# Decoder layer kernel: where the opening loads go, and which engine sums the second half of shift and scale

## The reference

```python
mod = (silu(c) @ w_ada + b_ada)             # c: (1, 1024), w_ada: (1024, 6144)
shift1, scale1, gate1, shift2, scale2, gate2 = jnp.split(mod, 6, axis=-1)

h = rms_norm(x, pre_mix_w) * (1.0 + scale1) + shift1
proj = h @ w_in                             # w_in: (1024, 2312)
q, k, v, xs, z, bm, cm, dt_raw = _split_last(proj, IN_SPLITS)
attn = sliding_window_attention(q, k, v, rel_bias, attn_sinks)
ssm = mamba2_mixer(xs, z, bm, cm, dt_raw, ...)
x = x + gate1 * rms_norm(concat([attn, ssm]) @ w_out, post_mix_w)

h = rms_norm(x, pre_ffn_w) * (1.0 + scale2) + shift2
u = causal_dwconv(h @ w_up);  f = gelu(u_gate) * u_val
x = x + gate2 * rms_norm(f @ w_down, post_ffn_w)
```

## Time and profile before

| | us |
|---|---|
| three runs | 1161.8, 1159.23, 1161.77 |
| median | 1161.77 |
| the profiled execution | 1160.59 |
| its span, from the first to the last instruction | 1158.8 |
| TensorE busy (share of the span) | 1100.1 (95%) |
| VectorE busy | 863.1 (74%) |
| ScalarE busy | 536.2 (46%) |

### The profile page before, as it was taken

How to read it: one execution, slowest core, us unless ns; L and a number is a source line. 1 busy time by engine, 2 the same in 40 slices (tenths; PEclk the granted TensorE clock), 3 DMA queues, 4 the chain that set the end, 5 groups by cost and what they waited for, 6 DMA issues and landing times.

```text
span 1158.8 us, 14802 instructions
## 1 busy us (share of the span) xinstructions
PE 1100.1 (95%) x5176; PEld 895.5 (77%) x5176; DVE 863.1 (74%) x1089; ACT 536.2 (46%) x900; POOL 212.1 (18%) x203
## 2 busy tenths in 40 slices
PE   2699999999999999969999999999999999999997
PEld 2578877777787878757888888888888888888885
DVE  5779567657459566587988888888888886776687
ACT  3631144445444343466454444454445454454453
POOL 2100000000012333123333333333333100000012
PEclk7699999999999999988999999999999999999999
DMA  9989311001132111105344343434353496733224
GB/s 341 313 245 316 119 37 37 20 19 37 37 110 81 64 38 55 56 36 146 109 164 140 131 151 120 159 128 158 109 170 109 144 365 225 237 100 98 94 90 165
DMA packets 115293, 152.69 MB, mean 132 GB/s; under 512 B 15084, under 2 KB 75053, under 8 KB 115245
## 3 DMA queue, kind: packets, MB, share of 16 engines
q1 hardware_dynamic: 114925, 151.00, 38.8%
q0 software_dynamic: 320, 1.06, 0.3%
HBM read 121.10 MB, written 30.95 MB: 131 GB/s over the span
## 4 chain that ended last, share of the span: by engine, by line
PE 89%; DVE 4%; DMA 2%; ACT 2%; issue 1%; POOL 1%; SPq 1%; DVEq 0%; POOLq 0%; ACTq 0%
PE ps L2259 34%; PE ps L1912 25%; PE ps L2324 17%; PE ps L1978 2%; PE ps L1951 2%; PE ps L1965 1%; PE ps L2102 1%; PE ps L2017 1%; DVE big L1233 1%; DMA raw<-in_w_in_dram 1%; ACT big L956 1%; DMA scratch<-in_rel_bias_dram 1%; PE ps L2146 1%; PE ps L2194 1%; PE ps L2094 1%
## 5 line engine op out<-in xcount | busy, mean ns | idle before, releaser
L1912 PE MATMUL ps<-a_hi,w_hi 128*128 128x512 f32 x416 | 144.8, 426 | 8.0 <-DVE a_lo L1293 5.7
L1912 PE MATMUL ps<-a_lo,w_hi 128*128 128x512 f32 x416 | 132.4, 397 | 0.0
L1912 PE MATMUL ps<-a_hi,w_lo 128*128 128x512 f32 x416 | 131.3, 394 | 0.0
L2324 PE MATMUL ps<-w_hi,a_hi 128*128 128x512 f32 x308 | 119.9, 389 | 0.2 <-DVE a_lo L1745 0.2
L2324 PE MATMUL ps<-w_lo,a_hi 128*128 128x512 f32 x308 | 119.8, 389 | 0.0
L2324 PE MATMUL ps<-w_hi,a_lo 128*128 128x512 f32 x308 | 119.8, 389 | 0.0
L1145 ACT ACTIVATE w_hi<-raw 128x512 fp32r<-128x512 f32 x77 | 48.7, 632 | 98.4 <-PE ps L2324 88.3
L1912 PEld LDWEIGHTS ps<-a_hi,w_hi 128*128 128x128 f32 x416 | 73.2, 191 | 26.5 <-issue 16.3
L1912 PEld LDWEIGHTS ps<-a_hi,w_lo 128*128 128x128 f32 x416 | 79.2, 190 | 18.2
L1912 PEld LDWEIGHTS ps<-a_lo,w_hi 128*128 128x128 f32 x416 | 78.9, 190 | 17.9 <-issue 0.5
L1065 ACT ACTIVATE scratch<-ps 128x512 f32<-128x512 f32 x88 | 52.2, 593 | 84.8 <-PE ps L2259 84.8
(11 more groups left out here) (244 smaller groups left out, 2418.1 us busy)
## 6 DMA issues: line engine op xcount, KB each, us to landing
big<-in_w_ada_dram SPq DMA_DIRECT2D x24, 1024.0 KB, 8.8
raw<-in_w_up_dram SPq DMA_DIRECT2D x22, 512.0 KB, 5.1
big<-in_w_up_dram SPq DMA_DIRECT2D x22, 512.0 KB, 4.7
big<-in_w_down_dram SPq DMA_DIRECT2D x22, 512.0 KB, 6.4
down_weight_sums<-big SPq DMA_DIRECT2D x22, 512.0 KB, 3.4
raw<-down_weight_sums SPq DMA_DIRECT2D x44, 256.0 KB, 2.8
ffn_hidden<-big SPq DMA_DIRECT2D x21, 512.0 KB, 2.6
big<-ffn_hidden SPq DMA_DIRECT2D x21, 512.0 KB, 7.5
```

The source lines that it names most:

```text
L1912: mm = pe.matmul(out, lhs_of[a], rhs_of(b, j), start=first and p == 0, stop=last and p == 2)
L2324: mm = pe.matmul(bk, a[:, ts], rhs_op(s)[w], start=fresh and m == 0, stop=last and m == 2, skip_group_check=s // KH in (J6, J3, J7))
```

## The change

**Places.** The eight blocks of x get places of their own in `spare` (the space of `a_hi` and `a_lo`, tiles 0 to 3 of each), and chunks 0 to 3 get four places: two in `big` as before, for chunks 0 and 2, and two in `spare` (tiles 4 to 7 of `a_hi` and `a_lo`) for chunks 1 and 3. No load of the opening waits for a consumer any more. SyncE's order is: x 0, constants, x 1, c, flip matrix, x 2 and 3, chunk 0, x 4 to 7, the small vectors, chunk 2, unit 0's weights, chunk 1, unit 1's weights, chunk 3, and, once the first columns are in PSUM, chunks 4 and 5.

**Halves.** Chunks 0 and 2 hold shift1 and scale1 of features 0 to 511, which are tiles 0 to 3 of h; chunks 1 and 3 those of tiles 4 to 7. VectorE sums chunks 0 and 2 in full, and tiles 0 to 3 are modulated after them (`take_part(0, 0)`). Of chunks 1 and 3 VectorE sums only rows j = 0 to 3, after the low halves of tiles 0 to 3. TensorE does the other four rows itself in `chunk_rows`: the four `silu(c)` columns, each beside a column of zeros (`c_pad`), are the stationary operand, the chunk's 512 columns stream, and one more product adds VectorE's partial sum; chunk 1 ends in the first and chunk 3 in the second of two PSUM partitions. ScalarE copies the two rows out (`copy_row`), TensorE turns them into columns (`row_columns`), VectorE takes them (`take_part(0, 1)`).

**Order of the steps.** TensorE does steps 0 to 3 of unit 0, the rows, steps 0 to 3 of unit 1 (the small transposes behind step 0), then steps 4 to 7 of unit 0 and of unit 1. The bias flips stand before step 6 of unit 1, where they stood before step 2. All transposes of x come first. ScalarE loads its table with a Silu of a constant and takes x's first squares before `silu(c)`.

**Names.** Some semaphores are joined: x blocks share theirs with the reloads of f (eight instead of six), chunk halves with the last stage's weights, and the four token sums of the feed-forward stage share one.

```diff
-        chunk = [flat(big[:, 4 * s:4 * s + 4, :]).rearrange("p (j n) -> p j n", j=KT) for s in range(2)]
+        chunk = [flat(tiles).rearrange("p (j n) -> p j n", j=KT)
+                 for tiles in (big[:, 0:4, :], big[:, 4:8, :], spare[:, 4:8, :], spare[:, 12:16, :])]
 
         x1nT = big[:, 0:8, :]
 
         def x_in(b):
 
-            return (raw if b % 4 < 2 else gate_rows)[:, b % 2, :]
+            return spare[:, b if b < 4 else b + 4, :]
...
+        c_pad = dtv[:, 0, 0:3 * KT].rearrange("p (j v) -> p j v", v=3)
+        one_pad = dtv[:, 0, 3 * KT:3 * KT + 3]
+        mod_row = scratch[0:2, 0:1024].rearrange("p (h n) -> p h n", h=2)
...
             load_x(0)
+            sp.dma_start(sq[:, :], squares[:, 0:3 * P]).then_inc(s_const, 16)
             load_x(1)
             sp.dma_start(ca[:, 0, :], c.rearrange("o (p j) -> p (o j)", j=KT)).then_inc(s_const, 16)
-            sp.dma_start(sq[:, :], squares[:, 0:3 * P]).then_inc(s_const, 16)
             sp.dma_start(flip, squares[:, 3 * P:]).then_inc(s_const, 16)
+            for b in range(2, 4):
+                load_x(b)
             load_chunk(0)
-            load_x(2)
-            load_x(3)
+            for b in range(4, NB):
+                load_x(b)
...
+            load_chunk(2)
+            load_in(0)
             load_chunk(1)
-            load_x(4)
-            load_x(5)
-            load_chunk(2)
-            load_x(6)
-            load_x(7)
+            load_in(1)
             load_chunk(3)
...
-                if n < 2:
-                    sp.wait_ge(s_xT, 5 + n)
-                else:
-                    sp.wait_ge(s_wlo, n - 1)
+            load_chunk(4)
+            load_chunk(5)
+            for n in range(2, U_OUT):
+                sp.wait_ge(s_wlo, n - 1)
                 if n != U_DT:
                     load_in(n)
...
             pool.wait_ge(s_bd, 16)
+            pool.wait_ge(s_mp, 2)
...
+            for b in range(4):
                 x_squares(b)
-                if b >= 3:
-                    x_evacuate(b - 3)
-            x_evacuate(NB - 3)
-            x_evacuate(NB - 2)
-            split_hi(0)
+                if b == 2:
+                    act.wait_ge(s_const, 48)
+                    act.activation(ca[:, 1, :], ca[:, 0, :], ACT.Silu).then_inc(s_cs, 1)
+                    act.wait_ge(s_cs, 1)
+                    act.wait_ge(s_pool, 5)
+                    act.activation(c_pad[:, :, 1], ca[:, 1, :], ACT.Copy).then_inc(s_cz, 1)
+            for b in range(3):
+                x_evacuate(b)
+            for b in range(4, NB):
+                x_squares(b)
+                x_evacuate(b - 1)
...
+            def copy_row(half):
+
+                act.wait_ge(s_rw, half)
+                act.activation(mod_row[:, half, :], bank(4 + half)[0:2, :], ACT.Copy).then_inc(s_rc, 1)
+
...
             h_hi(0)
             h_modulate(1)
-            for k in range(2, KT, 2):
-                h_modulate(k + 1)
-                h_hi(k - 1)
-                h_hi(k)
-            h_hi(KT - 1)
+            h_modulate(3)
+            h_hi(1)
+            h_hi(2)
+            h_hi(3)
+            split_hi(1)
+            copy_row(1)
+            act.wait_ge(s_mod, 2)
+            h_hi(4)
+            h_modulate(5)
+            h_hi(5)
+            h_hi(6)
+            h_modulate(7)
+            h_hi(7)
...
-            normalise(0)
-            normalise(1)
+            LOW = range(KT // 2)
+            for b in range(4):
+                normalise(b)
             sum_chunk(0)
-
+            for b in range(4, NB):
+                normalise(b)
 
             dve.wait_ge(s_rT, 1)
             link(dve.tensor_copy(cols[:, :], bank(7)[:, 0:280]))
...
-
-            sum_chunk(1)
-            normalise(2)
-            normalise(3)
             sum_chunk(2)
-            normalise(4)
-            normalise(5)
-            normalise(6)
-            normalise(7)
-            sum_chunk(3)
             dve.wait_ge(s_cols, 1)
...
             modulate(xnT, 0, 0, 0, T, s_h)
             split_lo(0)
-            for k in range(KT):
-                if k % 2 == 0 and k + 2 < KT:
-                    modulate(xnT, k + 2, 0, 0, T, s_h)
-                dve.wait_ge(s_hhi, k + 1)
-                h_lo(xnT, k, 0, T, s_hlo)
+            modulate(xnT, 2, 0, 0, T, s_h)
+            for k in range(4):
+                low_tile(k)
+            sum_chunk(1, LOW)
+            split_lo(1)
+            sum_chunk(3, LOW)
+            dve.wait_ge(s_mp, 2)
+            take_part(0, 1)
+            dve.wait_ge(s_mod, 2)
+            modulate(xnT, 4, 0, 0, T, s_h)
+            modulate(xnT, 6, 0, 0, T, s_h)
+            for k in range(4, KT):
+                low_tile(k)
...
+            def chunk_rows(half, v):
+
+                n = half + 2 * v
+                slot = ada_slot(n)
+                row = bank(4 + half)[0:2, :]
+                col = slice(1 - v, 3 - v)
+                pe.wait_ge(s_wb[2 * slot + 1], ada_loaded(n))
+                pe.wait_ge(s_cz, 1)
+                for j in range(KT // 2, KT):
+                    pe.matmul(row, c_pad[:, j, col], chunk[slot][:, j, :], start=v == 0 and j == KT // 2, stop=False)
+                pe.wait_ge(s_acc, 2 * half + v + 1)
+                mm = pe.matmul(row, one_pad[:, col], acc[:, n * 512:(n + 1) * 512], start=False, stop=v == 1)
+                if v == 1:
+                    mm.then_inc(s_rw, 1)
+
+            def row_columns(half):
+
+                pe.wait_ge(s_rc, half)
+                for f in range(4):
+                    c0 = EXT + 8 * half + 2 * f
+                    mm = pe.transpose(bank(6)[:, c0:c0 + 2], mod_row[:, half, f * P:(f + 1) * P], ident[0:2, 0:2])
+                mm.then_inc(s_mp, 1)
...
+            pe.wait_ge(s_pool, 5)
+            for b in range(NB):
+                x_transpose(b)
 
             pe.wait_ge(s_small, 16 * N_SMALL)
...
-            x_transpose(4)
-            sum_columns(2, EXT + 8)
-            x_transpose(5)
-            x_transpose(6)
-            x_transpose(7)
-            sum_columns(3, EXT + 12).then_inc(s_mp, 1)
+            part_columns(0)
+            part_columns(1).then_inc(s_mp, 1)
...
+
+            pe.wait_ge(s_xe, NB)
+            for k in range(KT // 2):
+                pe.wait_ge(s_wlo, 1)
+                pe.wait_ge(s_hlo, k + 1)
+                unit_step(0, k)
+            chunk_rows(1, 0)
+            chunk_rows(1, 1)
+            pe.wait_ge(s_wlo, 2)
+            for k in range(KT // 2):
+                if k == 1:
+                    row_columns(1)
+                unit_step(1, k)
+            for n in range(2):
+                for k in range(KT // 2, KT):
+                    pe.wait_ge(s_hlo, k + 1)
+                    if n == 1 and k == KT - 2:
+                        bias_flip()
+                    mm = unit_step(n, k)
+                mm.then_inc(s_wu, 1)
+
+            for n in range(2, U_OUT):
                 pe.wait_ge(s_wlo, n + 1)
...
```

More of the change, by code:

```diff
@@ new lines, in _, with load_in @@
+            in_src = w_in2.rearrange("(k p) n -> p k n", p=P)
+            def load_in(n):
+                dst = ring(raw, n).rearrange("p (k n) -> p k n", k=KT)
+                c0 = COLUMN[n] * P
+                if n < K:
+                    for e in range(2):
+                        h = n + 4 * e
+                        sp.dma_start(dst[:, :, e * HD:(e + 1) * HD],
+                                     in_src[:, :, h * HD:(h + 1) * HD]).then_inc(s_w[n % 2], 16)
+                else:
+                    sp.dma_start(dst, in_src[:, :, c0:c0 + P]).then_inc(s_w[n % 2], 16)
@@ L678, in _ @@
             pool.wait_ge(s_pool, 3)
-            for b in range(2):
+            for b in range(NB):
                 x_rstd(b)
@@ L683, in _ @@
             pool.dma_start(bias_d, ext_sb).then_inc(s_bd, 16)
-            for b in range(2, NB):
-                x_rstd(b)
             pool.wait_ge(s_bd, 16)
+            pool.wait_ge(s_mp, 2)
             for e in range(2):
@@ L1249, in _, with take_part @@
             dve.tensor_copy(ext_sb, bank(6)[0:H, 0:EXT]).then_inc(s_exs, 1)
-            sum_chunk(1)
-            normalise(2)
-            normalise(3)
             sum_chunk(2)
-            normalise(4)
-            normalise(5)
-            normalise(6)
-            normalise(7)
-            sum_chunk(3)
-            dve.wait_ge(s_cols, 1)
+            dve.wait_ge(s_cols, 1)
+            def take_part(n, half):
+                a = 16 * n + 4 * half
+                sums = bank(6)[:, EXT + 8 * half:EXT + 8 * half + 8].rearrange("p (f v) -> p v f", v=2)
+                for v in range(2):
+                    c0 = a + 8 * v
+                    ins = dve.tensor_tensor(modc[:, c0:c0 + 4], sums[:, v, :], cols[:, 8 * n + c0:8 * n + c0 + 4],
+                                            ALU.add)
+                link(ins)
+                dve.scalar_tensor_tensor(out=modc[:, a + 8:a + 12], in0=modc[:, a + 8:a + 12],
```

(2 more changed lines are left out.)

191 lines of the change are left out of this document (95 added, 96 removed).

## The result

| | before | after |
|---|---|---|
| median of four runs, us | 1161.78 (1159.23 to 1162.37) | 1167.92 (1167.04 to 1168.59) |
| the profiled execution | 1160.59 | 1167.04 |
| its span | 1158.8 | 1165.2 |
| first product of unit 0 | 52.62 | 44.05 |
| last low half of h done | 63.45 | 72.31 |

The ratio is 1.0048, 95% interval 1.0036 to 1.006: slower, by 6.1 us between the medians and 6.4 between the spans of the profiled executions. The gate products are 6.2 later, so nearly the whole loss is made by then; from there to the end the two kernels take 1025.3 and 1025.5 us (1158.8 - 133.49 and 1165.2 - 139.69).

A forecast was written before the change was run, and what follows sets the result against it. TensorE, busy nearly all the time, was taken as the bound. The larger of +2.5 and +5.9 us moved the profiled 1160.59 to 1166.5; with the median 1.2 above it, 1167.7 us, range 1164 to 1170.

The forecast's parts named there:

- First product: TensorE's start of unit 0: at 44.6 instead of 52.62, 8.0 us earlier, with bounds 39 and 47.
- Rival B: Opening: first product already at 40, everything moves by -4.6, 1163.1 us in all; chance 0.20.
- Row products: TensorE after step 3 of unit 0: ten products for chunks 1 and 3 at 0.86 each, 8.6 us.
- Rival D: Row products take one pass (0.227 each), opening early (38), low halves at 61.5, total 1157.0 us; chance 0.12.
- rival C: Granted clock falls in the ten row products, 1.72 each; price 8.6 us, total 1176 us; chance 0.10.
- Low halves done: Last low half of h, behind the second half of shift and scale: at 72.1, against 63.45 before.
- Unit 2: Start of unit 2 on TensorE: at 82.7 against 80.25 before, TensorE's own delay of +2.5 us.
- Unit 3's low weights: Split on VectorE: ready at 95.1 while unit 2 ends at 93.6, so TensorE waits 1.5 us.
- Columns: Column products of chunks 6 to 9 on TensorE: start at 118.9, +4.3 us.
- Chunk 11's sum: On VectorE: ends at 139.4 instead of 131.4, shifted by 8.0 us, while the gate products wanted 137.8.
- Gate products: Products that need chunk 11's sum: start +5.9 us later than 133.49, the sums' shift 8.0 less slack 2.1.
- The form of the answer: Final shift is the larger of TensorE's own (+2.5) and the sums' shift less their slack (8.0 - 2.1).

The follow-up runs named there:

- e7: After, with VectorE summing chunk 2 ahead of the copies of the vectors' columns and of the bias vectors; ratio to before 1.0023, span 1164.7 us.
- e3: After, with the eight row products of chunks 1 and 3 made twice into the same sums; ratio to before 1.0123, span 1173.5 us.
- e2: After, with the eight row products of chunks 1 and 3 left out, the two of the partial sums kept; ratio to before 1.0045, span 1164.4 us.
- e6: After, with VectorE summing chunks 1 and 3 in full and no row products; ratio to before 1.0088, span 1167.0 us.
- e4: After, with unit 3's weights issued as soon as their place is free, ahead of chunk 6; ratio to before 1.0014, span 1163.1 us.
- e5: e4, with VectorE summing chunk 4 in its idle time beside the rows and chunk 5 where chunk 4 was; ratio to before 1.0012, span 1163.0 us.
- e1: After, keeping only the opening loads' own places; loads, sums and products of the opening in the order of before; ratio to before 0.9977, span 1157.9 us.

## Why the prediction was right

Forecast 1167.7, measured 1167.92; the steps one by one:

- **First product**, 44.6: measured 44.05. Steps 0 to 3 of unit 0 then took 8.47 us (44.05 to 52.52) and not 7.75, as TensorE ran at half clock until 50.1; the two misses cancel, which is luck, so the rows began at 52.5 as forecast (52.35). The chain through normalise 7 was the bound and not the loads, as argued; e7 shows both. Rival B (40) is out.
- **Row products**, 0.86 each and 8.6 in all: measured 8.67 from the first to the next product of unit 1 (52.52 to 61.19), 0.87 on the margin (e3). Two output partitions cost as much as 128. This agrees with what the Trainium skill ("TensorE: Matmul & The Clock Gate", Part 3: Packing small matmuls) says of a matmul that uses little of the array. Rival D is out, and rival C too: the clock stood at 1.00 in the rows, and e2 and e6 show that it falls without them.
- **Low halves done**, 72.1: measured 72.31. **Unit 2**, 82.7: 83.07.
- **Unit 3's low weights**, 95.1 with a wait of 1.5: 95.9 and 1.70. **Columns**, 118.9: 119.96. Here the small misses add up to 1.1.
- **Chunk 11's sum**, 139.4: 139.6. **Gate products**, +5.9: +6.2.
- Hidden, but not foreseen: TensorE's own arrival at the gate products. I had it at 137.8, with the time that before took from the columns (18.82, a fall of the clock in it). It came 1.1 later at the columns and had no fall, 1.5 less, and was there at 137.35. Neither mattered for the end, since the sum of chunk 11 set the time; only the wait there became 2.34 instead of the 1 to 2 us of the forecast. Had the sums been in time, the forecast would have depended on a fall that comes or not; e4 is that case: of my two numbers for it the one without a fall was 1.9 off, the one with it 0.2.

The form of the answer is shown by e4 and e5 (take the sums' delay away and +2.5 is left), and the two parts' signs by e1. What isn't settled: why a fall is short, long or absent in a given run, and why the first feed-forward weights are in use 5.7 us after their issue in some runs and 7.1 in others (1.20 us of wait for TensorE in before, 3.40 in e1).

## What to carry to other kernels

Starting early on half of the data pays only if the other half then comes without new work for the engine that bounds the kernel. Here TensorE began 4.65 us earlier than with the places alone and then spent 8.67 on rows. Neither leaving the sums to VectorE (e6) nor filling VectorE's idle time (e5) mended that; the order of before with the places did. Measure the two halves of a change apart: the loads in places of their own gave 3.4 us that the split hid. And follow an early gain to the end: a load that takes longer from issue to use, and a granted clock that falls behind a run of tiny products or a wait, can take most of it back.
